# A two-block network on one core: attention's transposes a round later, its scaling a round sooner, rotation products a step sooner, the mixer's group norm in another order

## What is computed

```python
# block 1, mixer: y is 768 wide, in 4 groups of 192 channels
y = (y_f + flip(y_b) + d_skip * xs) * silu(z)
y = rms_norm(y.reshape(b, L, 4, 192), ssd_norm.reshape(4, 192))      # the group norm
out = concatenate([fourier_mix(u_f, fourier_w), y]) @ w_out

# block 2, twice (layers 0 and 1): four branches on the same input, three of them with softmax
yA = forgetting_attention(qA, kA, vA, ...)           # A: 8 heads, causal
yB = dsa_attention(rope(qB), rope(kB), vB, ...)      # B: 8 heads, the 256 best keys (or fewer)
yD = sliding_window_gqa(rope(qD), rope(kD), vD, ...) # D: 8 heads, a window of 128
yC = head_groupnorm(retention(rope(qC), rope(kC), vC)) * silu(gC)
merged = sum over n of sigmoid(gate_n) * (y_n @ w_branch[n]);  x = x + merged @ w_out
# rope turns pairs (x1, x2) of a head: x1*cos - x2*sin, x2*cos + x1*sin
```

## Time and profile before

| | |
|---|---|
| median of 3 runs | 3721.26 us (3715.21 to 3727.25) |
| the profiled execution's own time | 3724.43 us |
| its span | 3723.1 us |
| PE busy | 3510.5 us, 94% of the span |
| DVE, ACT, POOL busy | 1672.8, 1438.8, 1428.4 us |
| chain that ended last | 76% PE, 11% DVE, 5% ACT |
| granted clock of PE, mean | 0.967 |

### The profile page before, as it was taken

How to read it: one execution, slowest core, us unless ns; L and a number is a source line. 1 busy time by engine, 2 the same in 40 slices (tenths; PEclk the granted TensorE clock), 3 DMA queues, 4 the chain that set the end, 5 groups by cost and what they waited for, 6 DMA issues and landing times.

```text
span 3723.1 us, 45249 instructions
## 1 busy us (share of the span) xinstructions
PE 3510.5 (94%) x17424; PEld 2796.0 (75%) x17424; DVE 1672.8 (45%) x2997; ACT 1438.8 (39%) x2448; POOL 1428.4 (38%) x651
## 2 busy tenths in 40 slices
PE   6899999998799998999999999999998999999998
PEld 4788889785578886866676778887876766778886
DVE  7976463546420115845442243133754453234143
ACT  3223354554432223344443344343343443334342
POOL 3554433321244444334323444444333333344443
PEclk9999999999899998999999999999999999999999
DMA  7574355221122332212212222323222222223332
GB/s 300 193 248 145 126 160 166 69 86 51 46 74 91 102 91 81 90 62 82 78 64 91 86 79 89 103 90 110 82 72 71 71 74 89 76 85 95 98 95 81
DMA packets 118423, 376.45 MB, mean 101 GB/s; under 512 B 15424, under 2 KB 16320, under 8 KB 117952
## 3 DMA queue, kind: packets, MB, share of 16 engines
q1 hardware_dynamic: 107280, 356.33, 29.6%
q10 hardware_dynamic: 10928, 17.22, 1.6%
HBM read 359.86 MB, written 2.10 MB: 97 GB/s over the span
## 4 chain that ended last, share of the span: by engine, by line
PE 76%; DVE 11%; ACT 5%; issue 3%; POOL 2%; DMA 2%; ACTq 1%; SPq 0%; DVEq 0%; POOLq 0%
PE ps L1333 23%; PE ps L1334 22%; PE ps L1335 22%; DVE b L2194 2%; ACT b L1660 2%; PE ps L1576 1%; POOL b L2558 1%; PE ps L1597 1%; ACTq L1766 1%; PE ps L1558 1%; DVE b L2230 1%; PE ps L1631 1%; PE ps L1620 1%; PE ps L1554 1%; DVE b L2460 1%
## 5 line engine op out<-in xcount | busy, mean ns | idle before, releaser
L2558 POOL TENSOR_TENSOR b<-b,b 128x1024 fp32r<-128x1024 f32 (+2 forms) x579 | 1324.3, 2287 | 2183.2 <-ACT b L1660 2166.5
L1333 PE MATMUL ps<-b,b 128*128 128x512 f32 (+3 forms) x4848 | 1842.4, 380 | 75.1 <-POOL b L2558 29.2
L1334 PE MATMUL ps<-b,b 128*128 128x512 f32 (+3 forms) x4848 | 1803.4, 372 | 0.0
L1335 PE MATMUL ps<-b,b 128*128 128x512 f32 (+3 forms) x4848 | 1801.9, 372 | 0.0
L1333 PEld LDWEIGHTS ps<-b,b 128*128 128x128 f32 x4848 | 935.0, 193 | 309.7 <-issue 118.7
L1335 PEld LDWEIGHTS ps<-b,b 128*128 128x128 f32 x4848 | 934.1, 193 | 160.1
L1334 PEld LDWEIGHTS ps<-b,b 128*128 128x128 f32 x4848 | 935.4, 193 | 154.8 <-issue 5.1
L1660 ACT ACTIVATE b<-b 128x1024 fp32r<-128x1024 f32 (+2 forms) x622 | 607.4, 978 | 388.5 <-PE ps L1335 247.4
L2109 DVE SCALAR_TENSOR_TENSOR b<-ps,b,b 128x511 f32<-128x511 f32 x88 | 66.0, 750 | 365.0 <-ACT b L1711 365.0
L2194 DVE CUSTOM_DVE_ANT_0 b<-b,b,b 128x1024 bf16<-128x1024 f32 x112 | 218.7, 1953 | 16.1 <-DMA b<-in_ada 4.1
L1721 ACT ACTIVATE b<-b 128x512 fp32r<-128x512 f32 (+1 forms) x110 | 64.8, 590 | 397.4 <-DVE b L2118 294.7
(11 more groups left out here) (231 smaller groups left out, 2337.4 us busy)
## 6 DMA issues: line engine op xcount, KB each, us to landing
b<-in_w SPq DMA_DIRECT2D x458, 512.0 KB, 3.5
b<-in_ada SPq DMA_DIRECT2D x88, 512.0 KB, 5.2
b<-in_w SPq DMA_DIRECT2D x80, 384.0 KB, 3.1
b<-in_w SPq DMA_DIRECT2D x80, 320.0 KB, 2.9
b<-b ACTq DMA_DIRECT2D x176, 64.0 KB, 2.0
b<-in_const SPq DMA_DIRECT2D x24, 256.0 KB, 3.8
b<-in_x SPq DMA_DIRECT2D x1, 2048.0 KB, 16.4
out<-b SPq DMA_DIRECT2D x8, 256.0 KB, 2.5
```

What stands on the lines that cost most here:

```text
L1333: pe.matmul(out, a[0], b[0], start=first, stop=False)
L1334: pe.matmul(out, a[0], b[1], start=False, stop=False)
L1335: return pe.matmul(out, a[1], b[0], start=False, stop=last)
L2558: then(pool.tensor_tensor(wlo[j % NS][:, 0:nk * w], raw[j % NR][:, 0:nk * w], whi[j % NS][:, 0:nk * w].bitcast(F32), ALU.subtract), "lop", j)
```

## The change

Four edits. (1) `heads`: `s2` of a pair moves from round k-2 to k-3 and `s3` from k-3 to k-4, so that there are 20 rounds where there were 19; `sp2` is no entry of its own any more but the last part of each round, behind `s1`. (2) The rates fall, so that 20 entries take about as long as the 35 before. (3) Part 0 and part 1 of a rotation come one step sooner. (4) The group norm's steps are written out in another order, and its product uses bank 6.

```diff
@@ Fore.rope
-            self.tail = [None] * 5 + [dict(kind="rope", t=t, part=0), None, dict(kind="rope", t=t, part=1)]
+            self.tail = [None] * 4 + [dict(kind="rope", t=t, part=0), None, dict(kind="rope", t=t, part=1)]
@@ schedule, mixer
-    def groupnorm(hf, o):
-        own = (0, 1) if o == 0 else (2,)
-        done = (0,) if o == 0 else (1, 2)
-        return ([do("gn1", hf=hf, o=x) for x in own] + [do("gn2", hf=hf, o=o), do("gn3", hf=hf, o=o)]
-                + [do("gn4", hf=hf, o=x) for x in done] + [do("gn5", hf=hf, o=x) for x in done])
+    def gnorm(hf, *steps):
+        return [do(kind, hf=hf, o=o) for kind, o in steps]
...
-            B += [do("yv", k=k - 1)] + (groupnorm(0, k - 2) if k in (2, 3) else [])
-            if k == 5:
-                B += groupnorm(1, 0)[:2]
+            B.append(do("yv", k=k - 1))
+            if k == 3:
+                B += gnorm(0, ("gn1", 0), ("gn1", 1), ("gn1", 2))
+            elif k == 4:
+                B += gnorm(0, ("gn4", 0), ("gn4", 1), ("gn4", 2), ("gn5", 0), ("gn5", 1), ("gn5", 2))
+            elif k == 5:
+                B += gnorm(1, ("gn1", 0), ("gn1", 1))
+        if h == 9:
+            B += gnorm(0, ("gn2", 0), ("gn3", 0), ("gn2", 1), ("gn3", 1))
...
     part(F, tiles[2], range(5))
+    S += gnorm(1, ("gn2", 0), ("gn3", 0)) + [do("yv", k=5)] + weave(F)
+    S += gnorm(1, ("gn1", 2), ("gn2", 1), ("gn3", 1), ("gn4", 0), ("gn5", 0))
+    F = fore()
     for t in tiles:
         part(F, t, range(5, 6))
-    S += weave(F, groupnorm(1, 0)[2:] + [do("yv", k=5)] + groupnorm(1, 1), 1.1)
+    S += weave(F) + gnorm(1, ("gn4", 1), ("gn4", 2), ("gn5", 1), ("gn5", 2))
@@ heads
-            for k in range(len(PAIRS) + 3):
-                if 0 <= k - 2 < len(PAIRS):
-                    out.append(do("sp2", a=kind, l=l, w=k - 2))
-                out.append([do(s, a=kind, l=l, w=w) for s, w in (("s3", k - 3), ("s2", k - 2), ("s1", k))
+            for k in range(len(PAIRS) + 4):
+                out.append([do(s, a=kind, l=l, w=w) for s, w in (("s3", k - 4), ("s2", k - 3), ("s1", k), ("sp2", k - 2))
                             if 0 <= w < len(PAIRS)])
@@ rates
-        S += weave(F, heads("A"), 0.57) + [do("takey", l=l, o=0, t=t) for t in range(4)]
+        S += weave(F, heads("A"), 0.325) + [do("takey", l=l, o=0, t=t) for t in range(4)]
-        S += weave(F, heads("B"), 0.435) + [do("takey", l=l, o=1, t=t) for t in range(4)]
+        S += weave(F, heads("B"), 0.245) + [do("takey", l=l, o=1, t=t) for t in range(4)]
-        S += weave(F, heads("D"), 0.435) + [do("takey", l=l, o=2, t=t) for t in range(4)]
+        S += weave(F, heads("D"), 0.245) + [do("takey", l=l, o=2, t=t) for t in range(4)]
@@ number
         elif k == "gn2":
-            s["bank"] = gn_bank = take()
+            s["bank"] = 6
```

More of the change, by code:

```diff
@@ L874, in number @@
         elif k == "gn2":
-            s["bank"] = gn_bank = take()
+            s["bank"] = 6
             mark("gp", s["hf"], s["o"])
         elif k == "gn3":
-            s["bank"] = gn_bank
-            held[gn_bank] = False
+            s["bank"] = 6
             mark("gl", s["hf"], s["o"])
```

## The result

The changed kernel takes 3682.3 us (median of 4 runs, 3679.3 to 3685.7) where the kernel before takes 3720.2 (median of 4, 3715.2 to 3727.3): the ratio is 0.9899, 95% interval 0.9883 to 0.9915, 38 us less.

What follows compares the result with a forecast made beforehand. PE, busy 94% of the span, was taken as the bound, so its idle time and clock counted. Terms A -8.8, D -16.8, B +2, mixer -15.4 sum to -39.0: 3685, as a median 3682 us; range 3656 to 3714.

Steps and rivals of the forecast that it cites:

- Mixer, -15.4: Mixer: the group norm's new order takes out waits and low clock at its end and middle, 15.4 us less.
- the end: Mixer's end: PE goes on 4.6 us sooner after the last tiles, plus 1.3 us of low clock.
- the middle: Mixer's middle: waits before L1490 and L1530 and low clock shrink, some new waits come; together 9.5 us less.
- A, -4.4 a layer: Branch A: scaling issued a whole round ahead, so the wait before the transposes goes; 4.4 us less a layer.
- D, -8.4 a layer: Branch D: idle PE falls from 9.3 to 3.9 us and the clock's loss by 3.0; 8.4 us less a layer.
- The following: Tracing tiles in the new order: waits left of 3.9 us in D and 11.3 us in B.
- B, +2 for both layers: Branch B: eight rotated tiles in a row leave slightly more waiting than now; 2 us more for both layers.
- The rotation a step sooner (edit 3) does not shorten the wait for the transfers: Rotated tiles: transfers land unchanged, DVE only stands there 0.7 us earlier; counted inside the terms for B and D.
- rival (b): Branches: waits only move, perhaps through scalings held behind POOL; only the mixer gains; 3706 us, chance 0.20.
- (a): Branches: all waits go, since a scaling has a round to spare; -76 us, 3645 us, chance 0.12.
- Two signs that the prediction had set for (b) and (d): Branches: PE waiting before values' product or scores instead, or the gap between two copies in D over 10 us.
- (d): Branches: the rotation loop of 9.23 us a tile takes over, making the kernel slower; 3748 us, chance 0.07.

Runs made afterwards that it cites:

- x1: The kernel before with only the new order of the mixer's group norm, softmax branches as before: 3708.3 us, ratio 0.9959.
- z1: The changed kernel with the old rotation timing and the old density of rounds, leaving the new order and the new mixer: 3694.0 us, ratio 0.9932.
- x4: The kernel before with denser rounds alone; order, rotation and mixer as before: 3724.6 us, ratio 1.0010.
- y3: The kernel before with bank 6 for the group norm and the new order at the mixer's end alone: 3713.3 us, ratio 0.9989.
- x3: The changed kernel with the rotation's products a step later again, as in the kernel before: 3663.8 us, ratio 0.9846.
- z2: The changed kernel with the rotation as before and rounds denser by another 10 per cent: 3682.3 us, ratio 0.9897.
- y1: The changed kernel with the rotation's products two steps later: 3662.2 us, ratio 0.9848.

## Why the prediction came out right

The time was forecast to 0.3 us, and that closeness is luck: the sections fell by 41.7 us for the 39.0 of the sum, B came out 7 better than its term and D 4 worse, and medians of four runs that spread over 6 and 12 us are not known to 0.3. The mixer, A and the places of most waits were foreseen; one step was wrong by some 18 us, inside terms that came out nearly right.

*Mixer, -15.4: right in size and in place.* It measured -15.6 (changed) and -15.7 (x1), the end -5.6 for 5.9, the middle -10.1 for 9.5. The waits followed are there: 2.68 us for the output product behind tile 0's subtraction at 959.56 (2.9 forecast; of the end's terms, half of 12 times 0.2 us is 1.2, where the sum has 1.3), 1.9 at a bank before L1441 (1.8 forecast), 1.8 for the Fourier subtraction (2.2 forecast), and the 5.2 before L1490 gone; the one that is left before L1493 is 3.1, where "none above 3" was the sign.

*A, -4.4 a layer: right in size and in cause, but a condition was missing.* It measured -4.3 in both, 2.6 of it idle time. The step said "The scaling is issued a whole round ahead of the transposes [...] The wait before L1576 should go". The kernel before has one such wait in A, in the last round that still has scores:

```profile
1657.37 2.34 POOL L2558 TENSOR_TENSOR b<-b,b 128x1024 fp32r<-128x1024 f32 x1
1657.39 2.86 DVE L2182 TENSOR_TENSOR b<-b,b 128x512 f32<-128x512 f32 x1 [1.26 <-POOL b L2584]
...
1660.87 0.81 PE L1576 MATMUL ps<-b,b 128*128 128x128 f32 x4 [3.13 <-DVE b L2460]
```

A rotated tile's addition waits for POOL's cosine product and then takes 2.86 us beside the weight chunk's instruction (0.69 elsewhere), and the scaling stands behind it. In the new order the same transposes wait for nothing, in z1 as in the changed kernel. But with the new order alone A is 5 us longer than before (z1), since its last three rounds follow each other with no products between; with the density alone it is about as long as before (x4); with both 4.3 shorter. The density covers the end that the order makes longer, and the prediction gave it no part.

*D, -8.4 a layer: too large by 2.2.* It measured -6.3 and -6.1 (5.9 against the mean of six copies of the old order, in before, x1 and y3). The following left 3.9 us of waits; there are 5.5, since the bank's wait is 2.1 for 1.3 and one of 0.9 before pair 1's transposes had been missed. The 2.6 before pair 3's transposes came as 2.4. That is layer 0; in layer 1 the bank's wait is the same, but the wait before pair 1's transposes is 2.3 and the one before pair 3's 0.7.

*B, +2 for both layers: too high by 6 or 7.* It measured +0.8 and -5.8, -5.0 in all. The old order alone scatters from 141.2 to 147.6, mean 143.9; against that mean the new one is 2.0 shorter in each layer. The following left 11.3 us of waits; there are 8.9 and 9.3. Its places are right, but not both in one layer. Layer 0 has 5.4 us at pair 0's scaling (2.2 forecast), none at the bank, and 0.9 and 1.7 before the transposes of pairs 3 and 4 (3.2 and 1.9 forecast). Layer 1 has none at pair 0's scaling, 2.7 and 2.9 at banks behind L1760 (4.0 forecast), and 0.9 and 1.3 before pairs 3 and 4.

*"The rotation a step sooner (edit 3) does not shorten the wait for the transfers": the failed step.* True of the transfers: D's first sine product begins 4.5 us after its tile's copy with the edit and without it. But the price is at what stands behind. The prediction named it ("whatever fell in between now behind it") and counted only 0.7 us of DVE. In the new order it costs 18 us, in the old about 10. Because the two followings were made with edit 3 in, their sums held all the same; the waits that they left in D, at the bank and before pair 3's transposes, are 0 and 0.2 us in x3.

*The held instructions.* Beside POOL's weight chunk instruction (2.3 to 2.4 us) DVE's sine product takes 2.8 us in the rows of D, with edit 3 and without it; the addition before A's wait takes 2.9 and the scaling in x1 2.6. One more is in the changed kernel, at B's start in layer 0:

```profile
1676.54 2.48 DVE L2463 TENSOR_SCALAR b<-b,b 128x128 f32<-128x128 f32 x1
1676.58 2.35 POOL L2561 TENSOR_TENSOR b<-b,b 128x1024 fp32r<-128x1024 f32 x1 [2.28 <-ACT b L1663]
...
1679.16 0.45 PE L1579 MATMUL ps<-b,b 128*128 128x128 f32 x1 [4.47 <-DVE b L2463]
...
1711.42 0.29 DVE L2463 TENSOR_SCALAR b<-b,b 128x128 f32<-128x128 f32 x1
```

A 128x128 scaling takes 2.48 us, where the next tile's of this shape takes 0.29 at 1711.42, and TensorE's longest wait of the branches ends with it. The Trainium skill (SBUF — State Buffer, "Who interferes with whom") calls the port pair that DVE and GpSimd share an exclusive lock, which one of the two holds for its whole instruction. The traces agree with that. The page lets the order of issue decide who is blocked; by the start times of the profile this scaling and the one in x1 began 0.04 and 0.01 us ahead of POOL's instruction and were held all the same. A held scaling is not the general price that rival (b) feared: held scalings come in x3 too (one of 2.6 us at 1721.95), and TensorE waits for none of that length in its D.

*The rivals.* (a), all waits of the branches gone at 3645, was nearer than its 0.12 said: without edit 3 the kernel takes 3664, with little but B's start waiting. Two signs that the prediction had set for (b) and (d) did come, with the time as forecast: scores wait (2.1 us in each D, behind the copy), and one gap between two copies in D is 11.8 us. The gap was no good sign: x3 has one of 11.9 us, although its D waits so little. (d), the loop as the bound, did not come in the changed kernel; that it is what B pays for in x4 and z2 is argued, not shown.

The parts of the branches, with the new mixer throughout (the old order at the new density is x4's time less the mixer's 15.6; no run has it with the new mixer):

| | old density | new density |
|---|---|---|
| old order | 3708 | 3709 |
| new order, no edit 3 | 3694 | 3664 |
| new order, edit 3 | 3708 | 3682 |

Order and density are worth 14 us and nothing apart, and 44 together: the order takes waits out of a branch and leaves its end bare, the density covers the end.

The best version is the changed kernel with edit 3 left out (x3, 3664, or y1, 3662), 57 us under the kernel before.

## What to carry to other kernels

Where an engine works in order, ask what is queued directly behind an instruction that waits for a transfer, and not only how long it waits: one step of 0.7 us, which put rotated tiles' products ahead of rounds' scores, cost 5 to 7 us a branch. When a pipeline is made a stage longer, its last stages must still have other work between them; a rate that fitted the shorter one leaves them bare at the end. And where one edit of several is priced at nothing inside a following of the whole, follow the kernel once more without it: here that might have shown the better version before any run.

## What the runs showed of the hardware

That 0.2 us of phase between DVE and POOL decide over an instruction of 0.49 or 2.64 us had not been expected, nor that the instruction that begins first can be the one that is held. Over the twelve traces the line between the two is sharp. Eight scalings begin 0.00 to 0.05 us ahead of a weight chunk's instruction on POOL, by the profile's start times, and all take 2.5 to 2.6 us; the 39 that begin 0.06 to 0.27 us ahead take 0.3 to 0.5 us.

It goes with copies of the same code in one program that differ: B takes 141.2 to 147.6 us and D 127.7 to 133.3 over six copies in three kernels of the old order. B's were followed to the scaling of its fifth round in all three; D's spread was not. In the changed kernel A, B and D of the two layers agree within 0.2 us, although B and D wait in different places in the two layers; that was seen, not explained.
